# Hybrid encoder trunk on one core: the way from mixer to experts, taken by halves of the tokens

## The reference

```python
def rmsnorm(x, g):
    xf = x.astype(jnp.float32)
    y = xf * lax.rsqrt(jnp.mean(xf * xf, axis=-1, keepdims=True) + EPS)
    return (y * g.astype(jnp.float32)).astype(x.dtype)

def hier_moe(h, wg, bg, we, be, w1, w3, w2):      # h = rmsnorm(x, ffn_norm[layer])
    ...
    gprob = jax.nn.softmax((t @ wg).astype(jnp.float32) + bg.astype(jnp.float32), axis=-1)
    gval, gidx = lax.top_k(gprob, 1)
    elog = ((t @ we).astype(jnp.float32) + be.astype(jnp.float32)).reshape(T, MOE_GROUPS, MOE_PER_GROUP)
    elog = jnp.take_along_axis(elog, gidx[:, :, None], axis=1)[:, 0]
    eprob = jax.nn.softmax(elog, axis=-1)
    ev, ei = lax.top_k(eprob, MOE_TOPK)
    ...
    for e in range(MOE_EXPERTS):
        he = jax.nn.silu(t @ w1[e]) * (t @ w3[e])
        y = y + gate[:, e:e + 1] * (he @ w2[e]).astype(jnp.float32)
```

## Time and profile before

| | |
|---|---|
| timed runs | 1389.59, 1391.82, 1391.87 us; median 1391.82 |
| profiled execution | 1390.67 us, span of its instructions 1388.6 us |
| busy share of the span | PE 83%, PEld 46%, DVE 27%, ACT 19%, POOL 2% |
| DMA | 453.57 MB, 327 GB/s over the span |
| chain that ended last | DMA 46%, PE 44%, DVE 6%, ACT 2% |
| mean granted clock of TensorE | 0.957 |

### The profile page before, as it was taken

How to read it: one execution, slowest core, us unless ns; L and a number is a source line. 1 busy time by engine, 2 the same in 40 slices (tenths; PEclk the granted TensorE clock), 3 DMA queues, 4 the chain that set the end, 5 groups by cost and what they waited for, 6 DMA issues and landing times.

```text
span 1388.6 us, 19854 instructions
## 1 busy us (share of the span) xinstructions
PE 1157.5 (83%) x8290; PEld 640.9 (46%) x8290; DVE 371.5 (27%) x933; ACT 266.4 (19%) x485; POOL 31.0 (2%) x45
## 2 busy tenths in 40 slices
PE   4988797997778777687999999979896778878777
PEld 2665645443334333343587776455442334333232
DVE  2247613111101011110555653351111101111011
ACT  2233403111111011110232454021110101111010
POOL 3002100000000000000000000000000000000000
PEclk9999897999999999999999999979999999999999
DMA  9530074999999999999952334438999999999997
GB/s 337 234 122 0 1 318 169 414 427 429 429 429 428 429 428 429 428 429 428 384 198 97 121 122 174 190 121 318 429 429 429 429 428 428 430 428 428 428 428 318
DMA packets 33698, 453.57 MB, mean 327 GB/s; under 512 B 4664, under 2 KB 5052, under 8 KB 6268
## 3 DMA queue, kind: packets, MB, share of 16 engines
q1 hardware_dynamic: 32380, 452.08, 78.1%
q0 software_dynamic: 576, 0.35, 0.2%
q10 hardware_dynamic: 704, 0.60, 0.2%
HBM read 451.97 MB, written 1.05 MB: 326 GB/s over the span
## 4 chain that ended last, share of the span: by engine, by line
DMA 46%; PE 44%; DVE 6%; ACT 2%; issue 1%; SPq 1%; DVEq 0%; ACTq 0%
DMA ring<-in_moe_units 45%; PE bank L721 9%; PE bank L641 8%; PE bank L671 5%; PE bank L419 4%; PE bank L835 4%; PE bank L661 3%; PE bank L569 2%; PE bank L621 2%; PE bank L427 1%; PE bank L792 1%; DMA vrow<-in_od_conv_b 1%; PE bank L597 1%; PE bank L779 1%; DVE xT L1486 1%
## 5 line engine op out<-in xcount | busy, mean ns | idle before, releaser
L641 PE MATMUL bank<-ring,xT 128*32 128x256 f32 x4096 | 273.6, 410 | 108.3 <-DMA ring<-in_moe_units 95.6
L641 PEld LDWEIGHTS bank<-ring,xT 128*32 128x32 f32 x4096 | 130.2, 112 | 259.3 <-DMA ring<-in_moe_units 151.9
L671 PE MATMUL bank<-ys,pgT 128*128 128x512 f32 x512 | 244.8, 622 | 0.0
L671 PEld LDWEIGHTS bank<-ys,pgT 128*128 128x128 f32 x512 | 95.9, 198 | 137.9 <-issue 121.3
L1491 DVE TENSOR_TENSOR he<-sg,bank 128x128 f32<-128x128 f32 x64 | 18.4, 287 | 421.2 <-ACT sg L1023 421.2
L721 PE MATMUL bank<-h,ring 128*128 128x256 f32 x576 | 130.4, 382 | 0.0
L721 PEld LDWEIGHTS bank<-h,ring 128*128 128x128 f32 x576 | 107.3, 190 | 18.5 <-issue 5.1
L1029 ACT ACTIVATE ys<-bank 128x512 f32<-128x512 f32 x64 | 38.2, 597 | 309.4 <-PE bank L661 309.4
L661 PE MATMUL bank<-ring,heT 128*32 128x512 f32 x512 | 66.0, 635 | 23.7 <-DMA ring<-in_moe_units 16.0
L1023 ACT ACTIVATE sg<-bank 128x128 f32<-128x128 f32 x64 | 17.7, 277 | 337.1 <-PE bank L641 337.1
L621 PE MATMUL bank<-sel,xn 128*128 128x128 f32 x512 | 67.7, 288 | 7.6 <-DVE sel L1476 7.6
(11 more groups left out here) (303 smaller groups left out, 935.8 us busy)
## 6 DMA issues: line engine op xcount, KB each, us to landing
ring<-in_moe_units SPq DMA_DIRECT2D x160, 2048.0 KB, 26.4
extra<-in_moe_units SPq DMA_DIRECT2D x32, 2048.0 KB, 30.7
ring<-in_od_in_units SPq DMA_DIRECT2D x10, 2048.0 KB, 13.5
ring<-in_ev_in_units SPq DMA_DIRECT2D x6, 2048.0 KB, 22.3
ring<-in_od_out_units SPq DMA_DIRECT2D x4, 2048.0 KB, 8.0
ring<-in_ev_out_units SPq DMA_DIRECT2D x2, 2048.0 KB, 9.0
x<-in_x SPq DMA_DIRECT2D x2, 512.0 KB, 6.7
out<-x SPq DMA_DIRECT2D x4, 256.0 KB, 2.1
```

What stands on the lines that cost most here:

```text
L641: last = mm(bank[4 + e % 2][32 * j:32 * j + 32, 0:256], xT[:, 4 * part + k, CAP * e:CAP * e + CAP], w[:, k, :, 256 * (j // 2) + j % 2:256 ...
L671: last = mm(bank[2 * t + h][:, :], pgT[:, e, t, :], ys[:, e % 2, 512 * h:512 * h + 512], start=False, stop=closed)
```

## The change

Four things, each for both layers:

- **hT by halves.** PE turns half 0 into two banks of its own, four k in each, and half 1 into two others. DVE evicts k 0 to 3 and ACT k 4 to 7 of a half in one instruction each, unscaled. The router's products wait half by half, and for each half after four k. The norm's weights are multiplied into the router's weights `wr` instead, once, near the start of the program.
- **The root.** ACT squares and sums x, half by half, in place of DVE. The root is now computed on DVE from the bits of the number and three Newton steps (`root`, which the mixer of layer 1 already uses).
- **First selection.** `sel` and `pg` of step 0 are made from the ranks and gates themselves, before the rounds are counted, not from POOL's tables.
- **Step 0 outside the loop** on PE, DVE and ACT; the register is loaded after it and the loop starts at 1.

```diff
@@ PE: moe, before the experts @@
-                norm_transposes(n)
-                hT_ready(n)
-
-                pe.wait_ge(in_small, 16 * 4)
+                raw_transposes(n)
+
+                pe.wait_ge(wr_ok, 1)
                 for t in range(NT):
                     for k in range(KT):
+                        if k % 4 == 0:
+                            pe.wait_ge((hT_v, hT_a)[k // 4], 2 + 2 * n + t + 1)
                         last = mm(bank[4 * layer][:, 36 * t:36 * t + 36], hT[:, k, P * t:P * t + P], wr[:, layer, k, :], start=(k == 0), stop=(k == KT - 1))
...
-                pe.wait_ge(rt_ok, layer + 1)
-                last_step = pe.value_load(rounds[0:1, 2 + layer:3 + layer], min_val=NGROUPS - 1, max_val=ROUNDS * NGROUPS - 1)
...
-                with pe.Fori(0, last_step) as i:
+                step(0, False)
+                pe.wait_ge(rt_ok, layer + 1)
+                last_step = pe.value_load(rounds[0:1, 2 + layer:3 + layer], min_val=NGROUPS - 1, max_val=ROUNDS * NGROUPS - 1)
+                with pe.Fori(1, last_step) as i:
                     step(i, False)
@@ ACT: moe @@
-                norm_take(n, V_FFN + 8 * layer)
-                norm_root_both(n)
+                for t in range(NT):
+                    act.wait_ge(x_new, HT_NEW[n] + 2 * t + 2)
+                    fn(xn[:, t, :], x[:, t, :], ACT.Square, accum_out=st[:, t:t + 1]).then_inc(sq_ok, 1)
+                    act.wait_ge(hT_ps, 4 * n + 2 * t + 2)
+                    fn(hT[:, 4:8, P * t:P * t + P], bank[HT_BANK[n] + 2 * t + 1][:, :].rearrange("p (k t) -> p k t", k=4), ACT.Copy).then_inc(hT_a, 1)
...
@@ DVE: start of the program @@
+            dve.wait_ge(in_small, 64)
+            for l in range(2):
+                for k in range(KT):
+                    last = ts(wr[:, l, k, :], wr[:, l, k, :], vT[:, V_FFN + 8 * l + k:V_FFN + 8 * l + k + 1], None, ALU.mult)
+            last.then_inc(wr_ok, 1)
@@ DVE: moe @@
-                norm_take(n, V_FFN + 8 * layer)
-                dve.wait_ge(x_new, (4, 24)[layer])
-                norm(n, 1)
-                dve.wait_ge(var_ok, 2 * n + 2)
-                dve.wait_ge(root_ok, 2 * n + 2)
-                newton(st[:, 8:10], st[:, 6:8], st[:, 2:4], st[:, 10:12], (rms_ok, 1))
+                for t in range(NT):
+                    dve.wait_ge(hT_ps, 4 * n + 2 * t + 1)
+                    v_.tensor_copy(hT[:, 0:4, P * t:P * t + P], bank[HT_BANK[n] + 2 * t][:, :].rearrange("p (k t) -> p k t", k=4)).then_inc(hT_v, 1)
+                dve.wait_ge(sq_ok, HT_SQ[n] + 2)
+                ch.link(ts(st[:, 2:4], st[:, 0:2], 1.0 / D, EPS, ALU.mult, ALU.add))
+                root(8, 6, 2, 10, 2, (rms_ok, 1))
...
-                ch.link(v_.tensor_reduce(rr[:, 0:1], bank[5][:, 64:96], AX.X, ALU.max))
+                dve.wait_ge(ga_ok, 3 * layer + 3)
+                for t in range(NT):
+                    ins = stt(sel[:, 4 * t:4 * t + 4, :], bc(rk[:, t, 0:GROUP].unsqueeze(2), [P, GROUP, CAP]), 1.0,
+                              bc(iota.unsqueeze(1), [P, GROUP, CAP]), ALU.subtract, ALU.is_equal)
+                ins.then_inc(m["s_ok"], 1)
+                ch.put(v_.tensor_reduce(rr[:, 0:1], bank[5][:, 64:96], AX.X, ALU.max))
+                dve.wait_ge(m["s_ok"], 1)
+                for t in range(NT):
+                    ins = tt(pg[:, t, :, :, :], bc(sel[:, 4 * t:4 * t + 4, :].unsqueeze(2), [P, GROUP, 4, CAP]),
+                             bc(s32[:, 2, t, 0:GROUP].unsqueeze(2).unsqueeze(3), [P, GROUP, 4, CAP]), ALU.mult)
+                ins.then_inc(m["pg_ok"], 1)
```

More of the change, by code:

```diff
@@ L1013, in moe, with step @@
                 fn(arg[:, :, :], arg[:, :, :], ACT.Exp).then_inc(rt_ex, 1)
-                act.wait_ge(rt_ok, layer + 1)
-                nr = act.value_load(rounds[0:1, layer:layer + 1], min_val=1, max_val=ROUNDS)
-                with act.Fori(0, nr * NGROUPS) as i:
+                def step(i):
                     for b in range(2):
@@ L1033, in moe @@
                         take(e)
+                step(0)
+                act.wait_ge(rt_ok, layer + 1)
+                nr = act.value_load(rounds[0:1, layer:layer + 1], min_val=1, max_val=ROUNDS)
+                with act.Fori(1, nr * NGROUPS) as i:
+                    step(i)
             moe(0, 1)
@@ L1200, in newton, with root @@
                     ch.link(tt(y, y0, tmp, ALU.mult))
-            def root(y, y0, var, tmp, n):
+            def root(y, y0, var, tmp, n, done=None):
                 bits = st[:, :].bitcast(i32)
@@ L1396, in _ @@
             ins.then_inc(on_ok, 1)
-            residual(0, mo_acc[0])
+            residual(mo_acc[0])
             def moe(layer, n):
@@ L1506, in moe @@
                         take(e)
+                step(0)
+                nr = dve.value_load(rounds[0:1, layer:layer + 1], min_val=1, max_val=ROUNDS)
+                dve.wait_ge(tab_ok, 4 * layer + 4)
+                with dve.Fori(1, nr * NGROUPS) as i:
+                    tt(sel[:, :, :], bc(rtab[:, bass.ds(i, 1), :].rearrange("p a e -> p (a e)").unsqueeze(2), [P, 8, CAP]),
+                       bc(iota.unsqueeze(1), [P, 8, CAP]), ALU.is_equal).then_inc(m["s_ok"], 1)
+                    dve.wait_ge(m["s_ok"], i + 1)
+                    for t in range(NT):
+                        gt = gtab[:, bass.ds(i, 1), 4 * t:4 * t + 4].rearrange("p a e -> p (a e)").unsqueeze(2).unsqueeze(3)
+                        ins = tt(pg[:, t, :, :, :], bc(sel[:, 4 * t:4 * t + 4, :].unsqueeze(2), [P, GROUP, 4, CAP]), bc(gt, [P, GROUP, 4, CAP]), ALU.mult)
+                    ins.then_inc(m["pg_ok"], 1)
+                    step(i)
                 for h in range(2):
```

76 lines of the change are left out of this document (29 added, 47 removed).

## The result

| | before | changed |
|---|---|---|
| median of five timed runs, us | 1391.82 (1389.59 to 1394.83) | **1379.47** (1379.19 to 1381.66) |
| span of the profiled execution | 1388.6 | 1377.5 |
| ratio of times | | 0.9922, 95% interval 0.9904 to 0.9940 |

The changed kernel is faster by 0.78%, 10.9 us (8.4 to 13.4). The two medians lie further apart, 12.35 us; the ratio is taken over all the runs and not from the two medians. The forecast was 1383.7 us, a gain of 8.1 us. So the direction and the mechanism held, and the size was underrated.

The account below looks back on a forecast made before the run. Bytes bound the expert phases, so the path from mixer end to first release counts, once per layer. Savings of 2.5 + 1.7 and 2.5 + 1.45, together 8.1 us, gave 1383.7 us; range 1379.6 to 1388.5.

Parts of the forecast that it names:

- rival A: Whole kernel: more gained, with no POOL collision and PE keeping the high clock; gain 10 to 14 us, chance 0.16.
- Part 1: hT and router, transposes to scaled logits: plain evictions by halves start router products earlier, saving 2.5 us in each layer.
- 22 records until 921.1, ten at 0.224: Layer 1's router products: start 918.6, clock falls at 921.1 as before, the last ten records slow, end 923.3.
- with the high one throughout, layer 1 gains 3.4: Bound on layer 1's router products: at the high clock throughout, the gain is 3.4 us and the root is later.
- Part 2: Root on DVE by bits: ends before the router by 0.5 and 1.5 us, so it costs nothing while covered.
- The conditional sentence on the Exp table: Layer 1's Exp table load on ACT: barely covered; a router one microsecond earlier there would be held by it.
- ACT's Exp in layer 1 waits for DVE and not for its table: Expected sign in layer 1: table loaded by 927.4 us, before DVE's arguments for Exp at 927.7.
- Part 3: Ranks to gather: first selection from ranks takes 1.6 us, including 0.6 for colliding with POOL; saves 1.7 and 1.45 us.
- Gather to release: Link from PE's gather to the first ring release in each layer: stays at 6.8 and 7.3 us.
- rival B: Whole kernel: less gained, DVE held by both POOL instructions or clock rising later; gain 3 to 6.5 us, chance 0.24.
- Parts 4 and 5: Folding wr at program start, under 5.6 us in idle DVE time, and peeling step 0: neither costs anything.
- Rival D's point of decision: Loop entry behind step 0: stalls lose time from 4.8 us on, making the kernel slower; chance 0.05.

Follow-up runs that it names:

- C: Changed kernel with six linked DVE memsets of 1,024 columns between the ranks and the first selection in each layer; ratio to before 1.0021.
- A: Changed kernel with the first selection and peeled step 0 undone, leaving hT by halves, folded router weights and the root by bits; ratio to before 0.9957.
- B: Kernel before with only the first selection from the ranks and the peeled step 0 put in; ratio to before 0.9969.
- E: Changed kernel with POOL's tables held back until pg is made and a one-column Exp ahead of ACT's squares to load the table early; 1380.88 us, ratio 0.9915.
- G: Changed kernel with 40 products of zeros on PE between step 0 and the register load in each layer; 1391.07 us, ratio to before 0.9994.
- D: Changed kernel with 18 zero products on PE, ten ahead of the rank products and eight behind, to keep the clock high; 1379.25 us, ratio to before 0.9897.
- F: Changed kernel with PE's 18 zero products, POOL's tables held back until pg is made, and the early one-column Exp together; 1375.47 us, ratio 0.9871.

## Why the prediction was right, and where its sizes were off

The mechanism was right: two fixed expert phases, pushed forward by what is saved before the first release (C: one to one), in both halves of the change (A, B). The time, though, fell in rival A's range, to which the prediction gave 0.16. Of A's reasons one came true, the high clock through layer 1's router; the gather stayed at 3.75 us, and the collision with POOL exists. By the prediction's own steps:

- **Part 1, hT and router.** Forecast 2.5 us in each layer; T to logits shortened by 2.81 and 3.69. In layer 0 the 0.3 us are half an earlier start (T to router 2.47 us, against 207.66 - 205.03 = 2.63) and half that no record of the router ran at the low level. In layer 1 the step that failed is "22 records until 921.1, ten at 0.224": the prediction kept the moment of the clock's fall at its time of before. With everything earlier and PE's gap gone, all 32 records ran at 3.66 / 32 = 0.114 us (the 0.112 derived from the earlier trace rows was good), and the fall came behind them. The bound "with the high one throughout, layer 1 gains 3.4" was nearer the 3.69 measured, and it stood in rival A. This is the largest mis-sized term of the sum: 1.2 us. Its size hangs on the profile of before: with the old router T to logits was 10.03, 10.61 and, in B, 8.31 us in layer 1, with the new one 6.34 or 6.35 in all eight profiles. Which of the two, the earlier start or the missing gap, keeps the clock up is not shown.
- **Part 2, root by bits.** The root ended at 209.19 us against 209.75 for the last router product, the cover of 0.5 us that was forecast for layer 0. In layer 1 the cover was 0.6 us too, and not the 1.5 forecast, since the router ended earlier. It cost nothing. The conditional sentence on the Exp table came true: the router came over a microsecond earlier in layer 1, and the table held the exponentials for 0.59 us (E removes just that). What the prediction named as its sign, "ACT's Exp in layer 1 waits for DVE and not for its table", thus failed. The net of parts 1 and 2 in layer 1 is 3.1 us.
- **Part 3, first selection.** Forecast 1.7 + 1.45, measured 1.99 + 1.73. The collision with POOL exists, as the earlier trace rows suggested, and costs 0.42 us and not 0.6; a free pair takes 0.49 us and not the 0.66 taken. C and E show both. How the two collide is what the prediction read from its rows: an SBUF pair on DVE is held until POOL's running instruction ends, and POOL's is held in turn. The single instructions in layer 0 of the changed kernel, in the order in which they end (us):

| engine, instruction | starts | ends | behind the end of the other engine's last one | duration, and on a free engine (E) |
|---|---|---|---|---|
| DVE `sel`, t = 0 | 216.81 | 217.10 | | 0.29, 0.29 |
| POOL `rtab`, t = 0 | 216.86 | 217.58 | 0.47 | 0.72, 0.62 |
| DVE `sel`, t = 1 | 217.02 | 217.72 | 0.15 | 0.70, 0.28 |
| POOL `rtab`, t = 1 | 217.54 | 218.20 | 0.48 | 0.66, 0.62 |
| DVE `pg`, t = 0 | 217.76 | 218.75 | 0.55 | 0.99, 0.69 |
| POOL `gtab`, t = 0 | 218.15 | 219.00 | 0.26 | 0.85, 0.40 |
| DVE `pg`, t = 1 | 218.67 | 219.55 | 0.54 | 0.88, 0.68 |
| POOL `gtab`, t = 1 | 218.95 | 219.81 | 0.26 | 0.86, 0.40 |

  Each ends a fixed time behind the other engine's last one, by its kind. Layer 1 repeats these times within 0.01 us, and in the earlier trace rows DVE's 512-column pair ends 0.55 us behind POOL's instruction, as `pg` does here. So they take turns, instruction by instruction. What the prediction had wrong is the length of the hold: it took a whole POOL instruction, and POOL's first one had already run for part of its time, so 0.42 us were left.
- **Gather to release** was kept at its old length and grew by 0.53 us in layer 0 (0.09 in layer 1), since the clock rises later against the gather. The gather ran at the low level before too (3.79 us, now 3.75). Most of the difference is in `up(0, 0)`: 2.61 us at 222.51 above, 2.07 before, in the row below. This was in rival B, at 2 us per layer. In layer 1 the link has either size without any edit to it: 7.26 and 6.68 us in the two profiles of before.

```profile
228.73 2.07 PE L641 MATMUL bank<-ring,xT 128*32 128x256 f32 x32 [0.21 <-DVE xT L1486]
```

- **Parts 4 and 5** cost nothing, as forecast. Behind step 0 no gap is to be seen on PE; the first matmul of the loop starts as the last of step 0 ends:

```profile
263.71 3.70 PE L673 MATMUL bank<-ys,pgT 128*128 128x512 f32 x8
...
267.25 1.95 PE L623 MATMUL bank<-sel,xn 128*128 128x128 f32 x16
```

- **Rival D's point of decision** was given as 4.8 us, the difference of two landings. G puts it at 3.3 to 3.4. The conclusion stood, as the stall was nothing.

So the path gave 9.0 us where 8.1 were forecast. That accounts for 0.9 of the 4.2 us between 1383.7 and 1379.47. The other 3.3 us are outside the path. 1.2 of them are the step from the profile's span to the median: the profiled execution of before took 1.15 us less than the median, that of the changed kernel (1379.34) 0.13 less, and the two executions differ by 0.2 us more than their spans. 1.4 lie in mixer 0, and the longer phases take 1.0 back. The last 1.6 are at the end of layer 0.

The 1.4 us in mixer 0 come from its first products, which the change doesn't edit: they started 0.5 us later, but 96 of them took 33.30 us before and 31.28 in the changed kernel. The first four lasted 1.06 us or more in the one; in the other all but the first lasted 0.59, the length that they have at the high level in both.

```profile
22.70 33.30 PE L419 MATMUL bank<-ring,hT 128*128 128x512 f32 x96 [0.98 <-ACT hT L904]
```

```profile
23.18 31.28 PE L421 MATMUL bank<-ring,hT 128*128 128x512 f32 x96 [0.98 <-ACT hT L903]
```

The group took 33.1 to 33.6 us in both profiles of before, in B and in E, and 31.28 in the other seven. E has the changed router, so the early value doesn't come with it every time.

At the end of layer 0, from the last landing to the next norm, it is 8.0 us in both profiles of before and in A, 6.4 in both of the changed kernel and in B, D, E and F, but 8.0 again in C and G. It is TensorE's clock. Before and after, PE comes out of the same idle time and does the same products:

```profile
667.25 2.48 PE L661 MATMUL bank<-ring,heT 128*32 128x512 f32 x16 [1.14 <-DMA ring<-in_moe_units]
669.66 4.79 PE L671 MATMUL bank<-ys,pgT 128*128 128x512 f32 x8
```

```profile
662.27 1.92 PE L663 MATMUL bank<-ring,heT 128*32 128x512 f32 x16 [1.15 <-DMA ring<-in_moe_units]
664.15 3.70 PE L673 MATMUL bank<-ys,pgT 128*128 128x512 f32 x8
```

The granted clock stays 1.00 in the second and is 0.50 for some 3 us in the first. The same happens at the end of layer 1, and there both values occur in one kernel: the tail behind the last landing is 8.8 us in the first profile of before and 10.4 in its repeat, where the last products ran at a granted clock of 0.50 (10.4 also in B, C and E). So the value at an end of a layer can change from one execution to the next by itself. Whether the change has a part in the two gains outside the path, of 2.0 us in the first products and of 1.6 at the end of layer 0, stays open. The repeat of the changed kernel speaks for a part, as its 11.1 to 15.5 us lie above the path's 9.4 (the 8.4 to 13.4 of the first comparison don't); E for the first gain, and C and G for the second, speak against a fixed one. If the change does it, no term of the prediction held it.

## What to carry to other kernels

Where a phase is bound by bytes, find the first transfer that waits for computed work; the chain ahead of it is worth its length, once per layer, whatever the engines' busy shares are. When work on that chain moves earlier, don't leave TensorE's clock where it stood in the old trace: work it out at both levels and ask whether the new chain ends before the fall. And when one term gets shorter, look at once for the thing that was "barely covered" by it (here a table load of 1.28 us, and DVE's count behind a gather twice as fast).

## What the runs showed of the hardware

- A pair of `scalar_tensor_tensor` operations of 128 columns with two fp32 SBUF sources took 0.49 us on a free DVE and 0.91 beside two POOL operations; a pair of 512-column products 1.29 and 1.79. POOL's pairs took 1.19 and 0.74 free, 1.34 and 1.66 beside DVE. The two engines took turns: each instruction ended a fixed time behind the end of the other engine's last one, 0.15 us (DVE, 128 columns), 0.55 (DVE, 512 columns), 0.47 (POOL's `rtab`) or 0.26 (POOL's copy).
- With 18 extra products on PE (4.2 us of work in layer 1) the granted clock was 1.00 at the gather, which took 2.02 us instead of 3.75: without them, with PE idle ahead of it, it cost 1.7 us more.
- Products without any edit ran at either clock level from one execution to the next: at the program's start, in layer 1's old router, at the end of each layer. Each time that was 1.6 to 2.3 us.
- A DMA queue that ran dry was back at its full rate only some 3 us after the next issue, in both layers; 1.7 to 1.8 us' worth of transfer was missing there. This start has to be taken off the cover that a queue gives.
- The first pass of PE through the loop's code, register load included, showed no idle time.
